# Block 2: the value projection in halves of 512 columns, from two pairs of weight tiles each

## The chip, the cores and the metric

One core of a Trainium2 chip runs the whole program. The metric is the device time of one execution, in microseconds; the time shown is the median of three runs. A TensorE matmul is written PE here, its weight load PEld, VectorE is DVE, ScalarE is ACT, GpSimd is POOL, and SP issues the DMAs.

## The reference, cut to what matters

The program computes two blocks, one behind the other, on x of 512 tokens and 1024 features, all in fp32. The first block is a mixer of softmax attention and a gated delta rule with a gated projection behind it. The second block has two layers:

```python
for i in range(2):
    h = rms_norm_2(x, attn_norm[i])
    if i % 2 == 0: mix = stick_breaking_mixer(h, w_in[i], w_out[i])     # 16 heads of 64
    else:          mix = diff_mixer(h, positions, w_in[i], w_out[i], ...) # 8 heads of 2*64, partial rope
    x = x + mix
    x = x + swiglu_ffn(rms_norm_2(x, ffn_norm[i]), w_gate[i], w_up[i], w_down[i])
```

In either layer w_in has 3072 columns: q, k and v of 1024 columns each. Attention is causal: stick-breaking weights in layer 0, the difference of two softmaxes in layer 1. The change concerns v = h @ w_in[:, 2048:3072] of both layers.

## The kernel before, in words

**Precision and the weights.** A product of fp32 matrices is made of three matmuls in the type fp32r: high part by high part, high by low, and low by high. The weights come in 149 tiles ("pairs") of 128 partitions by 2048 columns, each a DMA of 1 MB into `raw`, in two buffers. Each is split in four pieces of 512 columns: ACT writes the high part (`w_hi`), DVE the low part (`w_lo`), both into `spl`, also in two buffers. A pair can be split only when the matmuls of the pair before the last are done, since they read the same half of `spl`.

**Main matmuls.** Activations stand with features on the partitions (`hh` and `hl`, high and low, 8 tiles of 128x512). A block of a pair is a 128x128 piece of weights; `mul` steps hold it in the array and move 512 tokens past it. 8 blocks of 3 matmuls make one output tile of 128 features, and a pair has 16 blocks, so 48 matmuls. The value projection (`gemm_tok`, steps `tok`) is the other way about, because v is needed with tokens on the partitions: a 128x128 piece of `hh` or `hl` is held in the array and the weights move past it. Before, one pair holds 256 columns of v for all 8 contraction tiles; for each of four blocks of 128 tokens (`tb`) 24 matmuls of 256 columns fill half a PSUM bank, and `v_out` scales it into `v8`. Four such pairs make v of a layer. `V_BEHIND` tells behind which tiles m of q and k they stand: 0, 2, 4, 6 in layer 0 and 1, 3, 5, 7 in layer 1. The pair behind is split at the second block of tokens (`tb == 1`).

**The order.** `arrange` writes out one list of steps, and each engine issues its own steps in the order of that list. Main matmuls run through; lanes (one generator for each kind of side work, named in `LANES`) put steps between them when the clock that the planner keeps of each engine lets them in. The numbers in `LANES` (rank, slack, lag, tie) and the costs above (`CHANGE`: what a change between fp32r and fp32 matmuls is thought to cost) decide this. Where a main step needs an operand that no lane has made yet, `until` forces lanes on, so that all steps up to that operand stand in the list before the next main matmul.

**Attention of layer 0.** For each tile m (two heads): `st_q`, `st_k` take q and k out of PSUM, `st_z` ... `st_l` (front lane) and `st_w`, `st_t`, `st_x`, `st_f`, `st_o`, `st_a` (back lane) run over four key blocks. `st_o` multiplies with v and waits for `v_out` of that head's columns. `os_hi` (ACT) and `os_lo` (DVE, line 2627) split the result for the output projection.

**Attention of layer 1.** For each m: `br_in` (DVE line 2823), a DMA that turns rows (`br_dma`), `br_ss` (PE), `br_rot` (2834), `br_out` (2839, 2844); then for four query blocks `df_s` (PE, and a maximum on DVE, 2848), `df_p` (2855, 2859, 2861, 2863), `df_t` (transposes on PE, copied by DVE 2871 or ACT), then `df_o` (PE, with v), `df_n` (PE) and `df_out` (2877). Again `os_hi` and `os_lo`.

**Output projection.** `out_proj` makes the 8 output tiles in two halves: first contraction tiles 0 to 3 for all 8 outputs (96 matmuls), then 4 to 7; for outputs 0 and 1 the tile k = 7 comes last, behind 18 matmuls. In layer 1 the operand tile 3 lies in a buffer that the rope lane uses, so `split_lane` lets `os_hi`/`os_lo` of tile 3 and up run only behind `br_out` of k of tile 7.

## Time and profile before

| | us |
|---|---|
| median of 3 runs | 2134.86 |
| lowest, highest | 2133.43, 2135.09 |
| the profiled execution | 2137.93 |
| its span | 2136.1 |
| PE busy | 2099.5 (98%) |
| DVE busy | 1256.4 (59%) |
| ACT busy | 1066.0 (50%) |
| POOL busy | 228.8 (11%) |
| DMA, all queues | 87 GB/s mean, 186.89 MB |

The span runs from the first to the last instruction of one profiled execution. PE busy counts a matmul from its recorded start to its end, and matmuls overlap in the array: the pace of a stream is read from start to start, not from the length of one. The granted TensorE clock was 0.998 of full speed on average, that is the level of 2.4 GHz nearly throughout.

### The profile page before, as it was taken

Reading aid. Unit: us, or ns where it says so; the run is one execution under the profiler, and the core shown is the slowest. Engines: PE = TensorE matmul, PEld = TensorE weight load, DVE = VectorE, ACT = ScalarE, POOL = GpSimd, SP = SyncE. Lnnn points to the kernel's source line nnn. Section 1 sums busy time; section 2 is a strip of 40 time slices with the busy share of each in tenths; the row PEclk is TensorE's granted clock in tenths of the full one; section 3 lists DMA queues with packets and bytes.
Section 4 is the critical chain, followed back from the end, with each engine's and each line's share of the span. In section 5 each row is a group of like instructions: output and inputs, shape, how many; then the busy total and the mean of one; then the engine's idle time right before and its main releaser. Section 6 shows DMA issues by size and latency. Waiting matters only on the chain.

```text
span 2136.1 us, 36010 instructions
## 1 busy us (share of the span) xinstructions
PE 2099.5 (98%) x15046; PEld 1678.5 (79%) x15046; DVE 1256.4 (59%) x2218; ACT 1066.0 (50%) x2094; POOL 228.8 (11%) x240
## 2 busy tenths in 40 slices
PE   7999999999999999999999999999999999999999
PEld 6777877877778887877777888888777778888887
DVE  6776767766755555655567443444677775443442
ACT  6766756766755236656664332333455554322331
POOL 1213221322120010100011000000111101000000
PEclk9999999999999999999999999999999999999999
DMA  4322222121224332111112222222212112232222
GB/s 182 109 66 81 71 74 81 66 89 52 71 75 157 120 138 98 60 60 60 60 60 80 100 102 85 93 99 99 84 64 65 65 66 94 98 112 85 99 103 76
DMA packets 36227, 186.89 MB, mean 87 GB/s; under 512 B 4560, under 2 KB 4944, under 8 KB 16992
## 3 DMA queue, kind: packets, MB, share of 16 engines
q1 hardware_dynamic: 36064, 184.58, 25.2%
q8 instruction: 119, 1.95, 0.4%
q14 instruction: 44, 0.36, 0.1%
HBM read 173.00 MB, written 7.90 MB: 85 GB/s over the span
## 4 chain that ended last, share of the span: by engine, by line
PE 90%; DVE 5%; ACT 3%; issue 1%; DMA 0%; SPq 0%; POOL 0%; DVEq 0%; ACTq 0%
PE ps L1930 89%; PE ps L1933 1%; ACT arena L2882 1%; DVE spl L2388 1%; ACT spl L2885 1%; ACT hh L2882 0%; DVE x L2748 0%; DMA raw<-wstream 0%; DVE hl L2699 0%; DVE arena L2407 0%; DVE arena L2691 0%; DVE x L2677 0%; DVE arena L2673 0%; ACT arena_r L2882 0%; ACT pad L2882 0%
## 5 line engine op out<-in xcount | busy, mean ns | idle before, releaser
L1930 PE MATMUL ps<-hh,spl 128*128 128x512 f32 (+1 forms) x3152 | 1014.4, 395 | 7.1 <-DVE hl L2699 1.6
L1930 PEld LDWEIGHTS ps<-hh,spl 128*128 128x128 f32 x3152 | 585.9, 188 | 138.1 <-issue 14.8
L1930 PE MATMUL ps<-hl,spl 128*128 128x512 f32 (+1 forms) x1568 | 617.1, 394 | 0.0
L2388 DVE TENSOR_TENSOR spl<-raw,spl 128x512 fp32r<-128x512 f32 x596 | 422.1, 733 | 137.3 <-ACT spl L2885 136.0
L1930 PE MATMUL ps<-arena_r,spl 128*128 128x512 f32 x1968 | 466.8, 391 | 8.9 <-DVE arena_r L2400 8.4
L1930 PEld LDWEIGHTS ps<-arena_r,spl 128*128 128x128 f32 x1968 | 370.2, 188 | 89.9 <-issue 11.6
L2885 ACT ACTIVATE spl<-raw 128x512 fp32r<-128x512 f32 x596 | 344.6, 618 | 144.4 <-PE ps L1930 139.0
L1930 PEld LDWEIGHTS ps<-hl,spl 128*128 128x128 f32 x1568 | 295.2, 188 | 61.6 <-issue 6.4
L2882 ACT ACTIVATE arena<-arena 128x512 f32<-128x512 f32 (+3 forms) x204 | 132.1, 649 | 180.3 <-DVE arena L2753 139.4
L1930 PE MATMUL ps<-arena 32*32 32x32 f32 (+7 forms) x5664 | 216.4, 224 | 5.3 <-issue 5.1
L1930 PEld LDWEIGHTS ps<-arena 32*32 32x32 f32 (+4 forms) x5664 | 127.1, 115 | 80.1 <-issue 71.4
L2885 ACT ACTIVATE arena_r<-arena 128x512 fp32r<-128x512 f32 x64 | 40.4, 631 | 203.0 <-DVE arena L2760 193.6
L2748 DVE TENSOR_TENSOR x<-x,ps 128x512 f32<-128x512 f32 x64 | 43.8, 685 | 134.8 <-PE ps L1930 134.7
L2882 ACT ACTIVATE arena<-ps,small 128x512 f32<-128x512 f32 (+3 forms) x126 | 71.0, 566 | 87.9 <-DVE small L2848 45.7
L3369 POOL TENSOR_TENSOR arena<-arena 128x512 f32<-128x512 f32 x29 | 38.6, 1331 | 615.8 <-ACT arena L2882 615.8
L2882 ACT ACTIVATE arena<-ps 128x512 f32<-128x512 f32 (+5 forms) x116 | 68.2, 600 | 71.0 <-PE ps L1930 68.7
L1930 PE MATMUL ps<-spl,hh 128*128 128x256 f32 x512 | 97.1, 290 | 0.0
L2757 DVE TENSOR_TENSOR arena<-ps,arena 128x512 f32<-128x512 f32 x44 | 30.4, 691 | 104.4 <-PE ps L1930 104.4
L1930 PEld LDWEIGHTS ps<-spl,hh 128*128 128x128 f32 x512 | 80.2, 191 | 7.2 <-issue 6.3
L2753 DVE TENSOR_TENSOR arena<-ps,arena 128x512 f32<-128x512 f32 x44 | 30.4, 691 | 77.1 <-PE ps L1930 74.7
L1930 PE MATMUL ps<-spl,hl 128*128 128x256 f32 x256 | 72.3, 282 | 0.0
L3358 POOL TENSOR_SCALAR kdt<-arena,small 128x128 f32<-128x128 f32 x48 | 38.4, 811 | 280.7 <-PE ps L1930 280.7
(272 smaller groups left out, 2138.3 us busy)
## 6 DMA issues: line engine op xcount, KB each, us to landing
raw<-wstream SPq DMA_DIRECT2D x148, 1024.0 KB, 4.9
arena<-spill SPq DMA_DIRECT2D x17, 256.0 KB, 5.5
GS<-g_rows SPq DMA_DIRECT2D x16, 256.0 KB, 3.8
spill<-x SPq DMA_DIRECT2D x14, 256.0 KB, 2.0
arena<-arena SPq DMA_DIRECT2D x18, 128.0 KB, 2.1
x<-xT SPq DMA_DIRECT2D x4, 512.0 KB, 6.2
spill<-arena SPq DMA_DIRECT2D x8, 256.0 KB, 2.0
x<-xT SPq DMA_DIRECT2D x1, 2048.0 KB, 7.6
```

Source lines behind the costliest of these rows:

```text
L1930: return pe.matmul(out, lhsT, rhs, start=start, stop=stop, skip_group_check=True)
L1933: return pe.transpose(out, in_, C["ident"])
L2388: tt(spl[:, p % 2, 1, c], raw[:, p % 2, c], spl[:, p % 2, 0, c].bitcast(F32), ALU.subtract) \
L2748: tt(X[q.m], X[q.m], psum[q.u.b][:, :], ALU.add).then_inc(drained[q.u.b], 1)
L2753: tt(f_sl[q.i], psum[q.u.b][:, :], SQ[q.name][2], ALU.mult).then_inc(drained[q.u.b], 1)
L2757: tt(p, psum[q.u.b][:, :], SQ[q.g.name][2], ALU.mult).then_inc(drained[q.u.b], 1)
L2882: return act.activation(out, in_, func, **kw)
L2885: return act.activation(out, in_, ACT.Copy)
L3358: i = po.tensor_scalar(kdt[:, d, :], g4(keep_of[q.keep]["kt"])[:, c, :], g3(edec)[:, c, col:col + 1], None, ALU.mult)
L3369: tt(acc, acc, tmp[q.i], ALU.add).then_inc(sem("sq_pool"), 1)
```

## The change

The value projection of either layer is made in two halves of 512 columns instead of four parts of 256. A half has 512 columns for 8 contraction tiles, which is two pairs of weights: pair p holds contraction tiles 0 to 3, pair p + 1 tiles 4 to 7. Two blocks of tokens go together: both through pair p (12 matmuls each, of 512 columns), then both through pair p + 1, and then the other two blocks of tokens the same way. A semaphore `pairs` tells that pair p is done, so that pair p + 2 can be split over it. Pair p + 1 is split at the first four steps, pair p + 2 at the last pass but one. The halves stand behind tiles 1 and 4 of q and k, in both layers. `v_out` takes 512 columns at once, 16 in all instead of 32. `st_o` and `df_o` of tiles 0 to 3 use the first half of v and those of tiles 4 to 7 the second.

`CHANGE` goes from 0.088 to 0.02, `vmm` joins the kinds that are counted as fp32r, and all 28 rows of `LANES` are new, so the order of the side work is another one in the whole program, block 1 included.

```diff
-V_BEHIND = ((0, 2, 4, 6), (1, 3, 5, 7))
+V_BEHIND = ((1, 4), (1, 4))
-CHANGE = 0.088
-ONE_PASS = ("mul", "tok", "ar_ss", "cv_r", "on_b", "st_w", "st_t")
+CHANGE = 0.02
+ONE_PASS = ("mul", "tok", "vmm", "ar_ss", "cv_r", "on_b", "st_w", "st_t")
-    'att': (5, 3, 0.3, 0),
+    'att': (5, 1, 1, 0.5),
...
     def gemm_tok(op, done):
         o.flush()
         p, b = divmod(o.block, 16)
-        assert b == 0
-        for tb in range(4):
-            if tb == 1:
-                split(p + 1)
-            o.until(main.ready)
-            u = main.take()
-            o.clock["PE"] = max(o.clock["PE"], u.t, o.pair_t[p])
-            for q in range(4):
-                st = o.main("tok", p, tb, q, cost=[("PE", 0.72)])
...
+        for tbs in ((0, 1), (2, 3)):
+            us = {}
+            for half in range(2):
+                for tb in tbs:
+                    if half == 0:
+                        o.until(main.ready)
+                        us[tb] = main.take()
+                    u = us[tb]
+                    o.clock["PE"] = max(o.clock["PE"], u.t, o.pair_t[p + half])
+                    for k in range(4):
+                        if (tb, half) == (0, 0):
+                            split(p + 1, [k])
+                        if (tb, half) == (2, 1):
+                            split(p + 2, [k])
+                        st = o.main("vmm", p + half, tb, k, cost=[("PE", 3 * MUL)])
+                        st.pair_mark = (half, tb, k) == (0, 3, 3)
...
+                elif kind == "vmm":
+                    u, j, c = q.u, q.p % 2, slice(q.tb * 128, q.tb * 128 + 128)
+                    w.wait_ge(sem("w_lo"), 4 * q.p + q.k + 1)
+                    n = slice(512 * q.k, 512 * q.k + 512)
+                    mm(o, hi[:, c], spl[:, j, 0, n], q.half == 0 and q.k == 0, False)
+                    mm(o, hi[:, c], spl[:, j, 1, n], False, False)
+                    i = mm(o, lo[:, c], spl[:, j, 0, n], False, q.half == 1 and q.k == 3)
...
-            while ("v_out", 0, kb, m // 2) not in o.at or not obs.ready():
+            while ("v_out", 0, kb, m // 4) not in o.at or not obs.ready():
-        while ("v_out", 1, 3, m // 2) not in o.at or not obk.ready() or not on_slot.ready():
+        while ("v_out", 1, 3, m // 4) not in o.at or not obk.ready() or not on_slot.ready():
```

**Place 1, PE, the first value projection of layer 0.** `hh,spl` and `hl,spl` are main matmuls of q and k, `cst,arena 128x1` is `rs_col`, `spl,hh` and `spl,hl` are the value projection, `arena 128x...` with `mask_b` a score of the stick-breaking attention. Before:

```order
L1930 MATMUL ps<-hl,spl 128x256
L1930 MATMUL ps<-hh,spl 128x256
L1930 MATMUL ps<-cst,arena 128x1 x4
L1930 MATMUL ps<-spl,hh 128x256 x2
L1930 MATMUL ps<-spl,hl 128x256
```

And changed:

```order
L1940 MATMUL ps<-hl,spl 128x512
L1940 MATMUL ps<-hh,spl 128x512 x2
L1940 MATMUL ps<-hl,spl 128x512
L1940 MATMUL ps<-hh,spl 128x512
L1940 MATMUL ps<-cst,arena 128x1 x4
L1940 MATMUL ps<-spl,hh 128x512 x2
L1940 MATMUL ps<-spl,hl 128x512
```

The projection now stands behind the 512-column matmuls of tile 1, not behind tile 0, which is made in halves of 256 tokens; its own matmuls have 512 columns.

**Place 2, PE, the start of the output projection of layer 1.** The operands `GS_r`, `rv_r` belong to contraction tiles 0 to 2 of the attention's output, `arena_r` to the low parts and to tile 3. `cst,arena 128x128` are transposes (`df_t`), `arena,cst`, `pad,cst` and `on_t,cst` the sums of `br_ss` and `df_n`, `arena 128x...` x2 with `mask_b` the scores `df_s`. Before, the last of the value projection and the first of the output projection:

```order
L1930 MATMUL ps<-spl,hh 128x256 x2
L1930 MATMUL ps<-spl,hl 128x256
L1930 MATMUL ps<-GS_r,spl 128x512
L1930 MATMUL ps<-arena_r,spl 128x512
L1930 MATMUL ps<-GS_r,spl 128x512
L1933 MATMUL ps<-cst,arena 128x128 x4
L1930 MATMUL ps<-GS_r,spl 128x512
L1930 MATMUL ps<-arena_r,spl 128x512
L1930 MATMUL ps<-GS_r,spl 128x512
L1930 MATMUL ps<-rv_r,spl 128x512
```

Changed, from the last matmul with tile 2 to the first with tile 3 (27 rows lie between the last `hh,spl` of k of tile 7 and that one, of which these are the last):

```order
L1940 MATMUL ps<-rv_r,spl 128x512
L1943 MATMUL ps<-cst,arena 128x128
L1940 MATMUL ps<-arena 128x256 x2
L1940 MATMUL ps<-mask_b 128x64 x2
L1940 MATMUL ps<-pad,cst 128x512
L1940 MATMUL ps<-arena 128x384 x2
L1940 MATMUL ps<-mask_b 128x64 x2
L1943 MATMUL ps<-cst,arena 128x128 x2
L1940 MATMUL ps<-arena 128x512 x2
L1940 MATMUL ps<-mask_b 128x64 x2
L1943 MATMUL ps<-cst,arena 128x128 x3
L1940 MATMUL ps<-on_t,cst 128x512
```

Before, the last 96 matmuls of the value projection lie between k of tile 7 and the output projection. Now the output projection starts right behind k of tile 7, and eleven rows of side work without a main matmul among them stand ahead of its tile 3.

On DVE, the end of what stands there from `br_in` of k of tile 7 to the `os_lo` of tile 3 that the same matmul needs: 29 instructions before, 25 changed. Before:

```order
L2848 TENSOR_REDUCE small<-ps 128x2
L2871 COPY arena<-ps 128x3x128
L2705 TENSOR_SCALAR arena<-ps,small 128x256
L2834 TENSOR_TENSOR on_t<-on_t,arena 128x512
L2855 RECIPROCAL small<-small 128x2
L2859 TENSOR_TENSOR small<-small 128x2
L2861 TENSOR_SCALAR arena<-arena,small 128x512
L2863 SCALAR_TENSOR_TENSOR arena<-arena,small 128x512
L2839 TENSOR_TENSOR pad<-pad,on_t 128x512
L2844 TENSOR_TENSOR arena<-pad 128x512
L2848 TENSOR_REDUCE small<-ps 128x2
L2627 TENSOR_TENSOR arena_r<-arena,arena_r 128x512
```

And changed:

```order
L2873 TENSOR_REDUCE small<-ps 128x2
L2859 TENSOR_TENSOR on_t<-on_t,arena 128x512
L2864 TENSOR_TENSOR pad<-pad,on_t 128x512
L2869 TENSOR_TENSOR arena<-pad 128x512
L2873 TENSOR_REDUCE small<-ps 128x2
L2880 RECIPROCAL small<-small 128x2
L2884 TENSOR_TENSOR small<-small 128x2
L2886 TENSOR_SCALAR arena<-arena,small 128x384
L2888 SCALAR_TENSOR_TENSOR arena<-arena,small 128x384
L2896 COPY arena<-ps 128x3x128
L2652 TENSOR_TENSOR arena_r<-arena,arena_r 128x512
```

The chain on DVE is of the same kinds and about as long; the weight splits and the `v_out` that stood in it are gone, and what PE has to do beside it is less.

**Place 3, PE, the last attention tile of layer 0 in the output projection.** `rv_r,const_r`, `st_r,const_r` and `arena_r,const_r 128x128` are `st_w` and `st_t` of tile 7, last key block; `arena 64x128 x2` is its `st_o`. `arena_r,spl` are the matmuls of the output projection. Before:

```order
L1930 MATMUL ps<-rv_r,const_r 128x128
L1930 MATMUL ps<-st_r,const_r 128x128
L1930 MATMUL ps<-arena_r,const_r 128x128 x2
L1930 MATMUL ps<-arena_r,spl 128x512 x5
L1930 MATMUL ps<-arena 64x128 x2
L1930 MATMUL ps<-arena_r,spl 128x512 x88
L1930 MATMUL ps<-hh,spl 128x512
```

And changed:

```order
L1940 MATMUL ps<-rv_r,const_r 128x128
L1940 MATMUL ps<-st_r,const_r 128x128
L1940 MATMUL ps<-arena_r,const_r 128x128 x2
L1940 MATMUL ps<-arena 64x128 x2
L1940 MATMUL ps<-arena_r,spl 128x512 x78
L1940 MATMUL ps<-hh,spl 128x512
```

The last 78 matmuls begin with k = 7 of outputs 0 and 1. Before, five matmuls stood ahead of `st_o` and ten between it and k = 7; now none stands at either place.

## Rows read from the trace of the kernel before

**Rows 1.** The page: busy time, share and instructions of PE; the chain by engine.

```profile
PE 2099.5 (98%) x15046; PEld 1678.5 (79%) x15046; DVE 1256.4 (59%) x2218; ACT 1066.0 (50%) x2094; POOL 228.8 (11%) x240
...
PE 90%; DVE 5%; ACT 3%; issue 1%; DMA 0%; SPq 0%; POOL 0%; DVEq 0%; ACTq 0%
```

**Rows 2.** Timeline of PE in a value projection: start, us, instruction.

```profile
1714.06 0.40 PE L1930 MATMUL ps<-spl,hh 128*128 128x256 f32 x2
...
1715.86 0.40 PE L1930 MATMUL ps<-spl,hh 128*128 128x256 f32 x2
```

**Rows 3.** Timeline of PE in the FFN, 512 columns, nothing between.

```profile
1805.27 0.39 PE L1930 MATMUL ps<-hl,spl 128*128 128x512 f32 x1
...
1808.67 0.39 PE L1930 MATMUL ps<-hl,spl 128*128 128x512 f32 x1
```

**Rows 4.** Timeline of PE ahead of the first value projection.

```profile
891.23 1.02 PE L1930 MATMUL ps<-cst,arena 128*128 128x1 f32 x8 [0.82 <-ACT arena L2882]
```

**Rows 5.** Windows: us, PE, PEld, DVE, ACT, POOL busy, clock, DMA share, GB/s.

```profile
1701.28:1719.97 18.69, 18.69 (x135) 15.48 (x134) 15.83 (x29) 9.77 (x25) 1.77 (x1) 1.00 0.19 60
```

**Rows 6.** Timeline of DVE in that stretch and just behind it.

```profile
1705.78 0.48 DVE L2705 TENSOR_SCALAR arena<-ps,small 128x256 f32<-128x256 f32 x1
1706.63 3.60 DVE L2388 TENSOR_TENSOR spl<-raw,spl 128x512 fp32r<-128x512 f32 x4 [0.37 <-ACT spl L2885]
...
1714.35 0.68 DVE L2834 TENSOR_TENSOR on_t<-on_t,arena 128x512 f32<-128x512 f32 x1
...
1716.01 0.75 DVE L2863 SCALAR_TENSOR_TENSOR arena<-arena,small 128x512 f32<-128x512 f32 x1
...
1718.95 0.42 DVE L2848 TENSOR_REDUCE small<-ps 128x2 f32<-128x256 f32 x1 [0.86 <-PE ps L1930]
1719.29 0.68 DVE L2627 TENSOR_TENSOR arena_r<-arena,arena_r 128x512 fp32r<-128x512 f32 x1
...
1720.97 0.35 DVE L2863 SCALAR_TENSOR_TENSOR arena<-arena,small 128x128 f32<-128x128 f32 x1
1721.89 0.29 DVE L2871 COPY arena<-ps 128x128 f32<-128x128 f32 x1 [0.57 <-PE ps L1933]
1722.79 0.69 DVE L2848 TENSOR_REDUCE small<-ps 128x2 f32<-128x512 f32 x1 [0.60 <-PE ps L1930]
```

**Rows 7.** Timeline of PE, layer 1: side work of each kind.

```profile
1702.60 0.92 PE L1930 MATMUL ps<-arena 64*128 64x384 f32 x4
...
1708.78 1.02 PE L1930 MATMUL ps<-pad,cst 128*128 128x512 f32 x2
1709.24 0.80 PE L1930 MATMUL ps<-spl,hh 128*128 128x256 f32 x2
...
1716.92 0.61 PE L1933 MATMUL ps<-cst,arena 128*128 128x128 f32 x4
1717.29 0.47 PE L1930 MATMUL ps<-GS_r,spl 128*128 128x512 f32 x1
...
1719.18 2.32 PE L1930 MATMUL ps<-arena 128*128 128x512 f32 x8
1721.26 0.49 PE L1930 MATMUL ps<-rv_r,spl 128*128 128x512 f32 x1
```

**Rows 8.** Timeline of PE and DVE, end of the attention of layer 0.

```profile
1126.70 1.71 PE L1930 MATMUL ps<-arena_r,spl 128*128 128x512 f32 x5
1126.80 0.53 ACT L2882 ACTIVATE arena<-ps 128x256 f32<-128x256 f32 x2
...
1128.34 0.44 PE L1930 MATMUL ps<-arena 128*64 128x128 f32 x4
1128.70 3.93 PE L1930 MATMUL ps<-arena_r,spl 128*128 128x512 f32 x16
...
1129.88 0.69 DVE L2627 TENSOR_TENSOR arena_r<-arena,arena_r 128x512 fp32r<-128x512 f32 x1
```

**Rows 9.** Windows: most of block 1.

```profile
50.00:600.00 550.00, 538.36 (x6831) 427.27 (x6831) 386.26 (x750) 375.58 (x783) 126.78 (x131) 0.99 0.23 77
```

More of the change, by code:

```diff
@@ L384, in gemm_tok @@
         p, b = divmod(o.block, 16)
-        assert b == 0
-        for tb in range(4):
-            if tb == 1:
-                split(p + 1)
-            o.until(main.ready)
-            u = main.take()
-            o.clock["PE"] = max(o.clock["PE"], u.t, o.pair_t[p])
-            for q in range(4):
-                st = o.main("tok", p, tb, q, cost=[("PE", 0.72)])
-                st.u, st.op, st.p, st.tb, st.q = u, op, p, tb, q
-                st.need = None if tb else [op.ready[k] for k in (2 * q, 2 * q + 1) if k not in op.seen]
-                op.seen |= {2 * q, 2 * q + 1}
-                if q < 3:
+        assert b == 0 and all(k in op.seen for k in range(KT))
+        for tbs in ((0, 1), (2, 3)):
[13 more added lines that the diff above has]
+                        st = o.main("vmm", p + half, tb, k, cost=[("PE", 3 * MUL)])
+                        st.u, st.op, st.p, st.tb, st.half, st.k = u, op, p + half, tb, half, k
+                        st.pair_mark = (half, tb, k) == (0, 3, 3)
+                        if k < 3:
+                            o.step()
+                    if half == 1:
+                        done(tb, u)
+                    elif tb == 3:
+                        o.n_pair_marks += 1
+                        o.pair_done[p] = ("pairs", o.n_pair_marks)
                     o.step()
-            done(tb, u)
-            o.step()
-        o.pair_done[p] = ("bank", u)
-        o.block += 16
+        o.pair_done[p + 1] = ("bank", u)
+        o.block += 32
     def low(op, k, kind, *key, then=None):
@@ L1226, in done @@
         def done(tb, u):
-            st = o.main("v_out", layer, tb, j, cost=[("AC" if tb % 2 else "DV", 0.4)])
+            st = o.main("v_out", layer, tb, j, cost=[("AC", AC_B) if tb % 2 else ("DV", DV_B)])
             st.u, st.tb, st.j, st.layer = u, tb, j, layer
@@ L1574, in arrange @@
         o.spawn("score", score_lane(m))
-        behind = [("df_out", m)] + [("br_out", "k", 7)] * (m > 2) + [("v_out", 1, 3, 3)] * (m == 7)
+        behind = [("df_out", m)] + [("br_out", "k", 7)] * (m > 2) + [("v_out", 1, 3, 1)] * (m == 7)
         o.spawn("split", split_lane("ob", ob, m, behind))
@@ L1979, in tensor @@
                         i.then_inc(filled[u.b], 1)
+                elif kind == "vmm":
+                    u, j, c = q.u, q.p % 2, slice(q.tb * 128, q.tb * 128 + 128)
+                    if q.k == 0 and q.half == 0 and u.n > 1:
+                        w.wait_ge(drained[u.b], u.n - 1)
+                    w.wait_ge(sem("w_lo"), 4 * q.p + q.k + 1)
+                    n = slice(512 * q.k, 512 * q.k + 512)
+                    hi, lo = HI[q.op.hi][4 * q.half + q.k], HI[q.op.lo][4 * q.half + q.k]
+                    o = psum[u.b][:, :]
+                    mm(o, hi[:, c], spl[:, j, 0, n], q.half == 0 and q.k == 0, False)
+                    mm(o, hi[:, c], spl[:, j, 1, n], False, False)
+                    i = mm(o, lo[:, c], spl[:, j, 0, n], False, q.half == 1 and q.k == 3)
+                    if q.pair_mark:
+                        i.then_inc(sem("pairs"), 1)
+                    elif q.half == 1 and q.k == 3:
+                        i.then_inc(filled[u.b], 1)
                 elif kind == "norm":
@@ L3133, in scalar @@
                         if k == 7:
-                            full(at["v_out", 1, 3, 3].u)
+                            full(at["v_out", 1, 3, 1].u)
                     copy(HI[name + "_h"][k], o8[k]).then_inc(sem("os_hi"), 1)
@@ L3474, in lay_out @@
             if m in V_BEHIND[i]:
-                tm(w, 2048 + 256 * V_BEHIND[i].index(m), 1)
+                c = 2048 + 512 * V_BEHIND[i].index(m)
+                for k in range(0, 8, 4):
+                    out.append(w[128 * k:128 * k + 512, c:c + 512].reshape(4, 128, 512).transpose(1, 0, 2).reshape(128, 2048))
         fm(a["w_out_2"][i], 0, 8, 0, OUT_FIRST)
```

68 lines of the change are left out of this document (34 added, 34 removed).

## The prediction

> **What bounds the kernel now.** I read the page first: PE is busy for 98% of the span, the next engine (DVE) for 59%, and the chain that ended last lies on PE for 90% [rows 1]. The reader is to see there that only two things change the time: the pace of PE's own stream, and the 36.6 us (2136.1 less 2099.5) in which PE stands still, so a microsecond saved on DVE or ACT counts only where PE waits for it. The timeline gives the pace of the two kinds of matmul that the change exchanges. Then I looked where PE waits now and where it would wait: at the first value projection, where attention ends in either layer, and in block 1. The order of the instructions tells what stands where; all durations are from the trace.
>
> **The value projection's own matmuls.** In a stream of 256 columns a matmul starts every 0.120 us: 15 of them between 1714.06 and 1715.86 [rows 2]. With 512 columns it is 0.227: 15 between 1805.27 and 1808.67 [rows 3], at full clock. Before there are 2 layers x 4 pairs x 96 = 768 matmuls of 256 columns, 768 x 0.120 = 92.2 us. Now there are 2 x 2 halves x 96 = 384 of 512, 384 x 0.227 = 87.2 us. All of it is on PE, so it counts in full: minus 5.0. The trace has no 512-column matmul with weights as the moving operand. The bounds are the rows' 0.227 and twice 0.120: a gain between 5.0 and 0. I take 5.0, because 256 columns cost the same 0.12 in either role in the rows I saw.
> For this exchange the Trainium skill (TensorE: Matmul & The Clock Gate, section Back-to-back issue gap) gives a spacing of N / 2.4 + 2.5 ns, so that only 2.5 ns per matmul is fixed. By it the gain would be 384 x 2.5 ns = 1.0 us; the rows have 120 and 227, so twice 120 less 227 is 13 ns, and the measurement decides.
>
> **The first projection no longer waits.** `rs_col` of layer 0 stands idle for 0.82 us for an ACT result of the norm [rows 4], since it follows tile 0 at once. Behind tile 1, 10.9 us (48 x 0.227) later, that result is old. Minus 0.8. `v_out` has half as many instructions, off the path: nothing.
>
> **Splits inside the projection.** Pair p + 1 must be split during the first 24 matmuls, 5.4 us, where before there was the whole of tb 1 to 3 (72 x 0.12 = 8.6 us). Four splits in a row took 3.60 us on DVE [rows 6], so 1.8 us is left for what stands between them on DVE and ACT. The wait is finer now (one piece of 512 columns at a time), which covers most. Eight such places (two per half): between 0 and 1 us each; I take 0.3 in all, with 8 as the bad end.
>
> **The start of the output projection in layer 1.** This is where I see a new wait. Before, the fourth value projection (96 x 0.12 = 11.5 us of PE) stands between k of tile 7 and the output projection. Now nothing does, and after nine main matmuls PE comes to contraction tile 3, whose `os_lo` is behind `br_out` of k of tile 7. It is the only place in block 2 where the order puts more than a dozen steps of DVE and ACT between two main matmuls.
> The chain on DVE: from `br_in` to that `os_lo` before took 18.69 us, 15.83 of them busy (85%), with PE never idle [rows 5]. Out of the 15.83 go the four weight splits (3.60) and two `v_out` (0.48 each), which leaves 11.3 [rows 6]. The softmax step there is of 128 instead of 512 columns (0.35 for 0.75, and I estimate 0.2 on the instruction ahead of it), and added are one `br_rot` (0.68), one copy (0.29) and a maximum of 512 for one of 256 columns (0.69 for 0.42): 11.3 - 0.6 + 1.24 = 11.9 us. It starts where the maximum of the first score of tile 6 is done. Ahead of that PE has five main matmuls (1.14), a sum (0.86), four transposes (0.45) and a score (0.6), 3.1 us, and the maximum takes 0.42: 3.5 us behind k of tile 7. So `os_lo` ends at 3.5 + 11.9 = 15.4 us if DVE never waits, and at 3.5 + 11.9 / 0.85 = 17.5 us if it waits as often as before.
> PE's work until then [rows 7]: nine main matmuls 2.0; three sums, each 0.86 (0.46 to the next start, whose record is 0.40 longer than usual), 2.6; ten transposes at 0.11 (four: 0.37 to the next start and 0.08 on its record), 1.1; `df_o` 2.08 and 0.09, 2.2; four scores, 384 columns at 0.92 and, by steps of 0.2 about it, 3.4. Together 11.3 us. PE waits 15.4 - 11.3 = 4.1 to 17.5 - 11.3 = 6.2 us. I take 5.2. Behind the waiting matmul stands the whole output projection, so nothing hides it; lanes that got ahead meanwhile save nothing later, since PE did not wait there before.
>
> **The end of attention in layer 0.** Before, five main matmuls stand ahead of the last `st_o` and ten behind it, ahead of k = 7. Now none does. Before: `st_w`/`st_t` end about 1126.9, `st_x`/`st_f` on ACT at 1127.33, `st_o` starts 1128.34 behind the five matmuls and is done by 1128.8, and `os_lo` ends at 1130.57 [rows 8]. Without them PE waits 0.5 us for ACT and then from the end of `st_o` to that of `os_lo`, 1130.57 - 1128.78 = 1.8. Together 2.3. The ends: 1.5, if `os_hi` and `os_lo` come without the 0.6 us split that stood ahead, and 3.5, if the scores are late as well.
>
> **The rest of the order.** The new lanes move all side work. The matmuls of block 1 are the same, and PE's idle time there is what can change: 550 - 538.36 = 11.6 us in the stretch from 50 to 600 us [rows 9]. I counted in the two lists of steps the places in block 1 where PE's side work stands behind a step of another engine with no main matmul between: 104 before, 86 now. In proportion 11.6 x 18 / 104 = 2.0 us less. The ends: 7 less (0.6 of it gone), 5 more, since such a list can just as well lose. PE changes between fp32r and fp32 work 375 times instead of 350. The 0.08 us that a main matmul behind transposes is longer on record [rows 7] is mostly theirs; I estimate 0.02 for a change: plus 0.4.
>
> **The sum.** -5.0 - 0.8 + 0.3 + 5.2 + 2.3 - 2.0 + 0.4 = +0.4 us. The profiled execution had 2137.93 us, its span 2136.1; the sum on it is 2138.3. The median of the runs is 3.1 us lower, so the forecast is 2134.86 + 0.4 = 2135.3 us.
>
> **Rivals.**
> *Block 1 gains more* (faster). The costs of the planner and the new lanes fit the chip better, and 7 of the 11.6 idle us go. For it: the 104 places that became 86, and that PE's idle time is spread over many short waits. Against it: the same lane numbers must serve both blocks, and the list of block 2 got a wait worse than any before. With the wait in layer 1 at its lower end (4.1): 2135.3 - 5.0 - 1.1 = 2129.2 us.
> *The chain in layer 1 takes what it took before* (slower). Its 25 instructions alternate with ACT, so taking the weight splits out of DVE need not shorten it: they filled gaps. If it takes 18.7 us again, PE waits 3.5 + 18.7 - 11.3 = 10.9 us instead of 5.2: 2141.0. It is slower than a measurement can miss as soon as the chain takes more than 17 us (wait 9.2). For it: 85% busy was with splits in the gaps. Against it: PE work between (scores, sums) came late before because main matmuls stood ahead of it, and now comes at once.
> *The splits are late* (slower). If each of the eight places costs 1 us, because maxima and softmax steps stand between them, 2135.3 + 7.7 = 2143.0. For it: DVE is 75 to 85% busy in layer 1. Against it: raw weights are long there, and each piece is waited for alone.
> *The 512-column form gains nothing*: weights as the moving operand at 0.24 each. Then 2140.3. Little speaks for it.
>
> **How the numbers follow.** A measurement of this kernel can tell 0.2%, 4.3 us, so "faster" is under 2130.6 and "slower" over 2139.1. Forecast as it stands, with its parts inside their bounds: 0.45. Block 1 gains more: 0.27. Chain as long as before: 0.15. Late splits: 0.09. No gain by 512 columns: 0.04. That gives 0.27 faster, 0.45 same, 0.28 slower. The likeliest case alone has a range of 2131 to 2139. For 8 in 10, I go down to the first rival's side, 2128, and up past the second rival to 2142.
>
> **What would show it.** The value projections have 384 matmuls of 512 columns, 0.227 apart: any other pace fails the first step. PE should show no wait for ACT ahead of `rs_col` of layer 0. PE should be idle for 4 to 6 us in short waits in the 18 us behind k of tile 7 of layer 1, the last of them ended by `os_lo` on DVE; if PE is busy there throughout, the main loss is wrong and the kernel is faster by 5 us. PE should be idle for 2.3 us at the end of the attention of layer 0. Idle time between 50 and 600 us should be near 9.6 us; far from it, the term that I know least has decided.

## The result, and the profile after

| | before | changed |
|---|---|---|
| median of 3 runs, us | 2134.86 | 2149.25 |
| lowest, highest | 2133.43, 2135.09 | 2146.03, 2149.97 |
| profiled execution, its span | 2137.93, 2136.1 | 2149.25, 2147.5 |
| PE busy | 2099.5 | 2097.7 |
| attention of layer 0 | 242.2 | 250.0 |
| attention of layer 1 | 239.7 | 248.4 |
| PE idle in layer 0's attention | 1.4 | 5.2 |
| PE idle in layer 1's attention | 2.5 | 11.2 |

The changed kernel is slower: the ratio of the medians is 1.0065, with an interval of 1.0051 to 1.0079. The forecast was 2135.3 with a range up to 2142.

The page of the changed kernel, the two rows that answer to [rows 1]:

```profile
PE 2097.7 (98%) x14662; PEld 1657.7 (77%) x14662; DVE 1262.6 (59%) x2210; ACT 1062.1 (49%) x2086; POOL 231.5 (11%) x240
...
PE 86%; DVE 7%; ACT 4%; issue 1%; DMA 1%; SPq 0%; POOL 0%; DVEq 0%; ACTq 0%
```

PE is busy 1.8 us less, but it stands still for 49.8 us (2147.5 - 2097.7) instead of 36.6, and of the 4% of the chain that PE lost, 3% went to DVE and ACT and 1% to DMA.

To find where, I took the start of the same main matmul in both traces, stage by stage. Block 1 takes 4.9 us less, the norm behind it 0.3 less, the attention of layer 0 (from the norm to the first output of contraction tiles 4 to 7) 7.8 more, the feed-forward network of layer 0 0.1 less, the attention of layer 1 8.8 more, and the rest the same: +11.3 on the profiled executions, whose times differ by 11.32. All of the loss is in the two attention stages.

**v.** The timeline of PE in the first projection (start, us, instruction), for [rows 2, 3], and the group of `rs_col`, for [rows 4]:

```profile
898.01 0.95 PE L1940 MATMUL ps<-cst,arena 128*128 128x1 f32 x8
...
900.45 0.62 PE L1940 MATMUL ps<-spl,hh 128*128 128x512 f32 x2
900.90 0.39 PE L1940 MATMUL ps<-spl,hl 128*128 128x512 f32 x1
...
902.26 0.39 PE L1940 MATMUL ps<-spl,hl 128*128 128x512 f32 x1
```

From 900.45 to 902.26 there are eight steps from start to start, 0.226 us each, and `rs_col` has no idle time ahead of it. Both steps came as forecast. The brackets below hold idle time only, from the recorded end of one matmul to the start of the next. A record is 0.16 us longer than the pace and the first matmul behind a wait takes about 0.1 more, so a wait costs 0.2 to 0.3 us beside its idle time.

**Layer 0.** The timeline of PE and DVE at the two places in the projections where PE waited; in brackets idle time and its releaser:

```profile
910.82 0.75 DVE L2730 TENSOR_SCALAR arena<-ps,small 128x512 f32<-128x512 f32 x1 [2.06 <-PE ps L1940]
...
911.72 1.08 PE L1940 MATMUL ps<-arena 128*64 128x512 f32 x4 [0.94 <-DVE arena L2730]
...
932.87 0.75 DVE L2730 TENSOR_SCALAR arena<-ps,small 128x512 f32<-128x512 f32 x1
...
933.76 0.65 PE L1940 MATMUL ps<-arena 128*64 128x256 f32 x4 [1.70 <-DVE arena L2730]
```

L2730 is `v_out`. The new order has a `st_o` as the very next PE instruction behind the last matmul of a block of v, so PE waits for DVE to take that block out of PSUM. In the second case DVE was also at weight splits and came to `v_out` 0.8 us after the block was done. At the end of the stage, for [rows 8]:

```profile
1130.09 0.44 PE L1940 MATMUL ps<-arena 128*64 128x128 f32 x4
...
1130.97 0.63 ACT L2910 ACTIVATE arena_r<-arena 128x512 fp32r<-128x512 f32 x1 [0.68 <-DVE arena L2768]
...
1131.63 0.69 DVE L2652 TENSOR_TENSOR arena_r<-arena,arena_r 128x512 fp32r<-128x512 f32 x1 [0.70 <-ACT arena_r L2910]
1132.37 3.91 PE L1940 MATMUL ps<-arena_r,spl 128*128 128x512 f32 x9 [1.84 <-DVE arena_r L2652]
```

This is the forecast wait: 2.0 us idle (0.12 and 1.84), where the forecast had 2.3. The kernel before had a wait of 0.5 us in this part, at 1125.8, so the term is 1.5 us net. Windows over it and over the wait at 933 (last columns: granted clock, DMA share, GB/s):

```profile
930.00:940.00 10.00, 8.30 (x34) 6.41 (x35) 5.71 (x13) 3.58 (x8) 0.42 (x1) 0.83 0.29 105
...
1131.00:1136.00 5.00, 3.63 (x9) 2.77 (x10) 2.03 (x4) 2.32 (x4) 0.00 (x0) 0.66 0.00 0
```

The granted clock is under 1: 0.83 over 10 us and 0.66 over 5 us are each 3.4 us at the lower level of 1.2 GHz, right behind a wait of 1.7 and of 1.8 us. In [rows 8] there was no wait. I had not thought of the clock at all.

Idle time in this stage is 5.2 us instead of 1.4, and 6.2 us at half clock lie inside it, worth 3.1 us at most. With v 2.5 us quicker, that makes 4.4 of the 7.8 us. The other 3.4 are in the stream itself. PE goes from main matmuls to those of `st_z` or `st_o` and back 55 times instead of 42. These use half of the array (`64*128` or `128*64` in the rows); e9 below has the price of such a visit. No edit in layer 0 shows that the 3.4 us are these 13 visits.

**Layer 1.** The timeline of PE from k of tile 7 (its last matmul starts 0.23 us ahead of the first row, which is the first matmul of the output projection) to contraction tile 3, for [rows 5, 7]:

```profile
1708.50 0.43 PE L1940 MATMUL ps<-GS_r,spl 128*128 128x512 f32 x1
1709.18 1.10 PE L1940 MATMUL ps<-arena,cst 128*128 128x512 f32 x2 [0.25 <-ACT arena L2907]
...
1714.90 0.48 PE L1940 MATMUL ps<-rv_r,spl 128*128 128x512 f32 x1
...
1716.08 1.13 PE L1940 MATMUL ps<-pad,cst 128*128 128x512 f32 x2
1717.99 0.92 PE L1940 MATMUL ps<-arena 64*128 64x384 f32 x4 [0.78 <-ACT arena L2907]
...
1720.39 0.44 PE L1943 MATMUL ps<-cst,arena 128*128 128x128 f32 x2 [1.46 <-DVE arena L2888]
1722.53 1.68 PE L1940 MATMUL ps<-arena 64*128 64x512 f32 x4 [1.69 <-ACT arena L2907]
...
1727.04 0.87 PE L1943 MATMUL ps<-cst,arena 128*128 128x128 f32 x3 [2.78 <-DVE arena L2888]
...
1729.16 0.83 PE L1940 MATMUL ps<-arena_r,spl 128*128 128x512 f32 x1
```

Four waits, 6.7 us, and 0.25 us at 1709, none of them for `os_lo` itself: PE's own side work (score, transposes, score, transposes) is part of the chain and is late each time, for an exponential on ACT or the end of a softmax on DVE. The two score matmuls on `64x512` took 1.68 us at half clock. DVE between, for [rows 6]:

```profile
1712.47 0.68 DVE L2848 TENSOR_TENSOR pad<-ps,arena 128x512 f32<-128x512 f32 x1
...
1717.21 1.40 POOL L3408 TENSOR_TENSOR pad<-pad,st 128x512 f32<-128x512 f32 x1 [3.49 <-DMA on_t<-pad]
1717.52 1.65 DVE L2869 TENSOR_TENSOR arena<-arena 128x512 f32<-128x512 f32 x1
...
1724.30 1.22 DVE L2873 TENSOR_REDUCE small<-ps 128x2 f32<-128x1024 f32 x1 [0.97 <-PE ps L1940]
...
1728.43 0.68 DVE L2652 TENSOR_TENSOR arena_r<-arena,arena_r 128x512 fp32r<-128x512 f32 x1
```

And the window from that `br_in` to that `os_lo`:

```profile
1712.47:1729.11 16.64, 9.92 (x40) 4.59 (x38) 13.05 (x27) 8.72 (x24) 2.65 (x2) 0.82 0.02 4
```

The chain took 16.6 us; it was 18.69 before [rows 5], but hidden. DVE was busy for 13.05 of it (78%), where the forecast had 11.9 and 85% at worst. 1.0 of the 1.1 us too much is one `br_out` (L2869): 1.65 us while POOL worked, 0.69 elsewhere. PE ran at half clock from 1723.0 to 1729.8, 6.8 us. From k of tile 7 to tile 3 it is 20.7 us (1729.16 less 1708.50). With the 11.3 us that the forecast gave to PE's own work, 9.4 us are lost, where it had 5.2: 7.0 us of idle time, and the rest clock, restarts and what 11.3 was short. Earlier in the stage three more waits of 0.95, 0.78 and 0.78 us stand at 1543, 1572 and 1656, which before did not have; the first is ahead of the first matmul of v, for a `br_in`.

**Block 1.** The window that answers to [rows 9]:

```profile
50.00:600.00 550.00, 537.88 (x6857) 429.37 (x6856) 397.66 (x755) 373.26 (x784) 129.64 (x133) 1.00 0.23 77
```

PE idles for 12.1 us, not for 9.6 as forecast and 11.6 before. What changed is the clock, 1.00 for 0.99: the execution profiled before had two pieces of 3.4 us at half clock (at 49.6 and 107.6 us), this one none. Two later executions of the same block 1 instructions without any, e8 and e11 below, were 4.0 and 2.9 us quicker in it than that profile. So 3 to 4 of the 4.9 us come and go between executions, and the order brought 1 to 2. That is also why the medians differ by 14.4 us and the profiles by 11.3.

### The profile page after: what moved, and what is told of

It is laid out like the page before. It is cut to its first block, busy times and chain, and to the rows that moved or that the text cites. A ratio compares the mean times of both kernels' runs of the same rounds, so it can differ in the third digit from the quotient of the medians.

```text
span 2147.5 us, 35252 instructions
## 1 busy us (share of the span) xinstructions
PE 2097.7 (98%) x14662; PEld 1657.7 (77%) x14662; DVE 1262.6 (59%) x2210; ACT 1062.1 (49%) x2086; POOL 231.5 (11%) x240
## 4 chain that ended last, share of the span: by engine, by line
PE 86%; DVE 7%; ACT 4%; issue 1%; DMA 1%; SPq 0%; POOL 0%; DVEq 0%; ACTq 0%
PE ps L1940 85%; ACT arena L2907 2%; PE ps L1943 1%; DVE spl L2413 1%; ACT spl L2910 1%; DMA arena<-spill 1%; DVE x L2773 0%; ACT hh L2907 0%; DMA raw<-wstream 0%; DVE hl L2724 0%; DVE arena L2432 0%; DVE arena L2716 0%; DVE x L2702 0%; DVE arena L2698 0%; ACT on_t L2907 0%
## 5 line engine op out<-in xcount | busy, mean ns | idle before, releaser
L1940 PEld LDWEIGHTS ps<-hh,spl 128*128 128x128 f32 x3152 | 584.3, 188 | 142.2 <-issue 14.4
L1940 PE MATMUL ps<-arena_r,spl 128*128 128x512 f32 x1968 | 471.6, 393 | 10.6 <-DVE arena_r L2425 8.4
L1940 PEld LDWEIGHTS ps<-arena_r,spl 128*128 128x128 f32 x1968 | 371.2, 189 | 95.3 <-issue 14.4
L1940 PE MATMUL ps<-spl,hh 128*128 128x512 f32 x256 | 84.0, 409 | 1.0 <-DVE pad L2848 1.0
L2910 ACT ACTIVATE arena<-ps 128x256 f32<-128x256 f32 (+2 forms) x88 | 39.3, 448 | 52.5 <-PE ps L1940 41.0
L1940 PEld LDWEIGHTS ps<-spl,hh 128*128 128x128 f32 x256 | 46.2, 189 | 17.5 <-issue 6.9
```

Of the source, the lines that this page charges most:

```text
L1940: return pe.matmul(out, lhsT, rhs, start=start, stop=stop, skip_group_check=True)
L2910: return act.activation(out, in_, ACT.Copy)
```

## The experiments

Two theories stood at the start. A: v's last block between k of tile 7 and the output projection was cover for the attention of tiles 5 to 7, and taking it away is the loss. B: the new lanes, made with a charge of 0.02 for a change of type, are the loss. The stage times below are those of one profile each, and waits are idle time as in the brackets.

### Width alone, and order alone (e1, e2)

e1 is the changed kernel with the old charge and lanes, e2 the kernel before with the new ones.

```diff
 e1, against the changed kernel
-CHANGE = 0.02
+CHANGE = 0.088
-    'att': (5, 1, 1, 0.5),
+    'att': (5, 3, 0.3, 0),
...
 e2, against the kernel before
-CHANGE = 0.088
+CHANGE = 0.02
-    'att': (5, 3, 0.3, 0),
+    'att': (5, 1, 1, 0.5),
...
```

> The changed kernel with the old LANES and the old CHANGE (0.088): the new value projection alone. The order again puts 22 steps of side work between two main matmuls in front of contraction tile 3 of the output projection of layer 1. Theory A (the place of v makes the wait there, and a wait that long halves TensorE's clock for a while): a wait of 7 to 11 us there, with a granted clock of 0.5 in it, and +3 to +9 us against before. Theory B (the new lane numbers are the fault): no slower than before, by the projection's gain 2130 us.

> The kernel before with the new LANES and CHANGE 0.02, and v as it was. Theory A: no wait in layer 1; block 1 is 4.9 us shorter as in the changed kernel; in all 2128 to 2134 us, unless the end of the attention of layer 0 (20 steps in one place in this order) costs 4 us and a dip of the clock. Theory B: +8 us or more against before.

e1: 2156.12 us, ratio 1.0099 (1.0084 to 1.0114). Layer 0 +4.7 us with 56 groups on half the array, layer 1 +16, with 11.0 us idle between 1716 and tile 3 at 1734.8 and 13.7 us at half clock from 1727.5 on. e2: 2154.72 us, 1.0090 (1.0075 to 1.0105): layer 0 +7.5 with 54 groups, layer 1 +12.5 with waits of 4.0 us at 1731 to 1733 and 2.1 at 1773. Each half of the change alone costs 19 to 20 us, both together 14. They don't add; the new lanes suit the new v better than the old lanes do, and neither is good. Neither theory stands alone. In e1 the wait of A came, in a total far above A's 3 to 9 us, and B fell. In e2 it is the other way: A had 2128 to 2134 us and B 8 us or more, and B came. There the last quarter of v still stands behind tile 7 and layer 1 is 12.5 us longer all the same, so the new lanes can lose as much in it with the cover in place.

### v's second half back behind tile 7 (e3)

```diff
-V_BEHIND = ((1, 4), (1, 4))
+V_BEHIND = ((1, 4), (1, 7))
```

> The changed kernel with the second half of v of layer 1 behind tile 7 of q and k instead of tile 4, so that 21.8 us of matmuls stand again between k of tile 7 and the output projection. Theory A: the wait of 8.8 us and the 6.8 us at half clock in front of contraction tile 3 go, 8 to 10 us faster than the changed kernel, about 2139 to 2141. Theory B (the wait only moves to where df_o of tiles 4 to 7 needs v): 3 us faster at most.

2168.31 us, 1.0155 (1.0140 to 1.0170), the slowest of all: layer 1 +27. The cover is there, but half a v is the columns of four tiles. `df_o` of tiles 4 to 7 now waits for it. PE waits 1.9, 3.5, 2.8 and 4.5 us at 1625 to 1699, as I read it because q and k find no free slot, and 8.2 us in four waits at 1771 to 1781. My expectation was wrong; the test changed more than the cover, and decides nothing on A.

### Spare matmuls in the waits (e4)

Matmuls of 320 columns whose results are overwritten, 10 and 19 of them, ahead of two of the transposes that waited.

```diff
+                    if m == 6 and qb in (1, 2):
+                        for _ in range(10 if qb == 1 else 19):
+                            mm(psum[u.b][:, 0:320], ones_r[:, :], const_r[:, :], True, True)
```

> The changed kernel with 29 spare matmuls of 320 columns (constants, into the bank that the transposes then overwrite) put in front of two transposes of tile 6 of layer 1, where PE waited 1.46 and 2.78 us: about 0.146 us each, so 1.5 and 2.8 us of work in place of idle time. If the half clock follows from PE being idle, the 6.8 us at 0.5 there shorten or go, and 1 to 3.4 us are won; if the loss is the chain on DVE alone, the time stays or grows by up to 1 us.

2146.93 us, 1.0051 (1.0034 to 1.0068), for 2149.25. The window of the stretch in e4:

```profile
1710.00:1731.00 21.00, 18.13 (x100) 12.20 (x99) 17.27 (x35) 12.94 (x34) 2.68 (x2) 1.00 0.03 6
```

The clock is 1.00 there, for 0.82, and the stage takes 1.3 us less (247.1). So the clock was worth about 1.3 us of the 9.4. The waits for the chain on DVE and ACT remain: tile 3 still comes 19.8 us behind k of tile 7.

### Buffers of their own for tiles 3 to 5 (e5, e7)

Theory C: it is only the dependence of `os_hi`/`os_lo` of tile 3 on `br_out` of k of tile 7, through a shared buffer.

```diff
-        behind = [("df_out", m)] + [("br_out", "k", 7)] * (m > 2) + [("v_out", 1, 3, 1)] * (m == 7)
+        behind = [("df_out", m)] + [("br_out", "k", 7)] * (m > 5) + [("v_out", 1, 3, 1)] * (m == 7)
-        HI["ob_h"] = [...] + [R(i) for i in (20, 21, 22)] + [...]
+        HI["ob_h"] = [...] + [R(i) for i in (41, 42, 43)] + [...]
...
-                        if k > 2:
+                        if k > 5:
                             w.wait_ge(sem("br_out"), 16)
```

> The changed kernel with contraction tiles 3, 4 and 5 of the output projection's operand of layer 1 in buffers of their own, so that their os_hi and os_lo wait only for their own df_out and not for br_out of k of tile 7. Theory A (the 8.8 us ahead of tile 3 are a false dependence through that buffer, made late by the place of v): they go, and of the 11.3 us that the output projection of layer 1 ends late at least 6 do; about 2141 to 2143 us, with some 2 us of a new wait at k = 7. Theory C (the attention of tiles 6 and 7 itself is late, whichever buffer it has): the wait moves to k = 7 with its full size and the time stays within 2 us of the changed kernel's.

2155.33 us, 1.0090 (1.0073 to 1.0107), 6 us slower than the changed kernel. PE passes tile 3 without a wait, and then waits for tiles 6 and 7, 9.2 us in six waits from 1748 to 1771 with 12.8 us at half clock. Two of them:

```profile
1751.48 0.44 PE L1943 MATMUL ps<-cst,arena 128*128 128x128 f32 x2 [1.10 <-DVE arena L2888]
...
1754.93 0.79 PE L1940 MATMUL ps<-pad_r,spl 128*128 128x512 f32 x1 [1.92 <-DVE arena_r L2652]
...
1766.30 1.13 PE L1940 MATMUL ps<-on_t,cst 128*128 128x512 f32 x2 [1.26 <-ACT arena L2907]
...
1770.98 0.79 PE L1940 MATMUL ps<-hh,spl 128*128 128x512 f32 x1 [3.55 <-DVE arena_r L2652]
```

The buffer is not the cause, since the loss does not go with it. Theory C had the time within 2 us of the changed kernel's; it came 6 us above. My reading, which no edit tests: what is late is the attention of the last tiles, and without the early stop the projection uses up the main matmuls under which it would have run. e7 is the same with the charge of 0.088:

> Both: tiles 3 to 5 in buffers of their own, and CHANGE 0.088. Theory A: neither the wait ahead of tile 3 nor that at the end of layer 0; 5 to 9 us faster than the changed kernel, 2140 to 2144 us, with about 2.5 us left at k = 7. If it comes under 2135 the value projection's 5 us reach the total.

2167.35 us, 1.0149 (1.0134 to 1.0164), layer 1 at 256.9 us, with 9.6 us of waits at 1760 to 1780 for the same tiles and 12.8 us at half clock. The forecast of 2140 to 2144 was far off.

### The charge alone (e6)

```diff
-CHANGE = 0.02
+CHANGE = 0.088
```

> The changed kernel with CHANGE back at 0.088. The order has 11 steps of side work in one place ahead of tile 3 (17 in the changed one) and none at the end of layer 0, and 58 groups of narrow matmuls (st_z, st_o) among the main ones of layer 0 instead of 55. If waits decide: 2 to 4 us gone at the end of layer 0 and 2 to 4 in layer 1, about 2142 us. If the number of groups decides, at 0.2 us each: +0.6 us in layer 0 beside that. If the order of block 1 decides: block 1 ends more than 3 us later or earlier.

2164.33 us, 1.0131 (1.0116 to 1.0146). Block 1 +11.1 us, layer 0 +3.6 (0.5 us of wait at its end), layer 1 +11.0. Of the three forecasts the one on block 1 came: the lanes were made for the charge of 0.02, and with another they give a poor order there.

### What a wait does to the clock (e8)

The kernel before, with 9 to 18 spare products on DVE ahead of five of the `f_g` of the dense feed-forward network of layer 1.

```diff
+                    for _ in range({(0, 2): 9, (0, 5): 11, (0, 8): 13, (1, 2): 18, (1, 6): 10}.get(q.key[1:], 0) if q.key[0] else 0):
...
+                        tt(A(41), A(42), A(42), ALU.mult).then_inc(pad_ops.sem, pad_ops.up())
```

> The kernel before with 9, 11, 13, 18 and 10 spare products of 512 columns on DVE ahead of five f_g of the FFN of layer 1, so that PE, otherwise dense there, stands still about 1, 2.5, 3.5, 6.5 and 2 us at five places. If idle time of PE alone brings the half clock, each gap over 2.5 us is followed by at least 3.4 us at 0.5, and the kernel is longer by the gaps and 1.7 us more for each 3.4 us at 0.5; the shorter gaps show where it begins. If only long mixed stretches bring it, the granted clock stays at 1.0 and the kernel is longer by the gaps alone, about 15 us.

One run, 2158.99 us. Two of the four waits in the timeline of PE in e8, and windows of 10 us behind them:

```profile
1804.36 0.47 PE L1930 MATMUL ps<-hh,spl 128*128 128x512 f32 x1 [2.24 <-DVE spl L2388]
...
1840.94 0.77 PE L1930 MATMUL ps<-hh,spl 128*128 128x512 f32 x1 [3.69 <-DVE spl L2388]
```

```profile
1836.00:1846.00 10.00, 6.31 (x21) 4.82 (x20) 7.27 (x12) 3.34 (x6) 0.00 (x0) 0.83 0.31 105
1802.00:1812.00 10.00, 7.76 (x35) 6.37 (x35) 6.08 (x10) 4.49 (x8) 0.00 (x0) 1.00 0.32 107
```

Behind 2.2 us of idle time the clock stayed, behind 3.7 us it was halved for 3.4 us, and with 5.1 and 6.2 us for 6.8 each, of which the first 2.1 us fell into the wait itself. The network took 25.5 us more, 17.8 of it idle. The other 7.7 go with 12.8 us in which PE worked at half clock: halving is 6.4 of them, and restarts behind four waits about 1. In the attention stages the clock fell after less: behind the wait of 1.7 us at 933 in three executions that share that stretch (the changed kernel, e4, e10), and not in two others (e3, e5), whose layer 0 was about 1.5 us quicker.

### What a group on half the array costs (e9)

The kernel before with spare fp32 matmuls of 128 columns ahead of 100 output tiles of the network, 1, 2 or 4 at a time.

```diff
+                        for _ in range(times):
+                            if form == 0:
+                                mm(o[:, 0:128], C["ident"][0:64, :], C["ones"][0:64, :], True, True)
+                            elif form == 1:
+                                mm(o[0:64, 0:128], C["ident"][:, 0:64], C["ones"], True, True)
+                            elif form == 2:
+                                mm(o[:, 0:128], C["ident"], C["ones"], True, True)
```

> The kernel before, with spare fp32 matmuls of 128 columns ahead of the first matmul of 100 output tiles of the feed-forward network (50 in each layer), in groups of 1, 2 or 4: on 64 rows of the array (as st_z), on 64 columns of it (as st_o), or on all of it. Theory (each return from a half array to the whole one costs about 0.2 us, whatever the size of the group): the time added at a start, set against the group's size, has an intercept of about 0.2 us for the two half forms and below 0.05 us for the whole one. Rival (it is the spare matmuls themselves, or the change of type, that cost): the intercept is the same for all three forms.

The timeline of PE in e9 round a pair of each form (an fp32 matmul has two records):

```profile
1158.78 0.39 PE L1930 MATMUL ps<-hh,spl 128*128 128x512 f32 x1
1159.10 0.71 PE L1930 MATMUL ps<-cst 64*128 64x128 f32 x4
1159.74 0.50 PE L1930 MATMUL ps<-hh,spl 128*128 128x512 f32 x1
...
1177.88 0.39 PE L1930 MATMUL ps<-hh,spl 128*128 128x512 f32 x1
1178.19 0.65 PE L1930 MATMUL ps<-cst 128*64 128x128 f32 x4
1178.78 0.50 PE L1930 MATMUL ps<-hh,spl 128*128 128x512 f32 x1
...
1196.56 0.39 PE L1930 MATMUL ps<-hh,spl 128*128 128x512 f32 x1
1196.78 0.60 PE L1930 MATMUL ps<-cst 128*128 128x128 f32 x4
1197.14 0.48 PE L1930 MATMUL ps<-hh,spl 128*128 128x512 f32 x1
```

From main matmul to main matmul it is 0.96, 0.90 and 0.58 us. Over all starts, the time added by 1, 2 and 4 spares (median of 8 to 10 each, over four main matmuls of 0.227 around them) is 0.63, 0.85, 1.30 us on 64 rows; 0.57, 0.81, 1.23 on 64 columns; 0.24, 0.46, 0.91 on the whole array. Every spare costs 0.22 in each form; what remains for the group is 0.40, 0.35 and 0.02. The form of the theory holds, its size does not: I had 0.2 us for a visit to half the array, and it is 0.35 to 0.40. A change of type costs 0.02 us, as I had it. The Trainium skill (TensorEngine Tiling (Array Packing), Key Properties) says that a change of the tiling mode drains the engine, and gives no price. By these, the 13 groups more in layer 0 would be 4.6 to 5.2 us; 3.4 are left for them there.

### A short softmax (e10, e11)

In both kernels the softmax of tiles 5, 6 and 7 of layer 1 works on a quarter of its columns (the rest is left out), in the same order.

```diff
-                    n, i = 128 * q.key[1] + 128, 2 * ((q.n - 1) % 8)
+                    n, i = (128 * q.key[1] + 128) // (4 if q.key[0] > 4 else 1), 2 * ((q.n - 1) % 8)
```

> The changed kernel, with the softmax of tiles 5, 6 and 7 of layer 1 on a quarter of its columns (VectorE and ScalarE work on 32 to 128 columns for 128 to 512; the rest is left out, the order stays). Theory (these tiles' chain on VectorE and ScalarE is what TensorE waits for ahead of contraction tile 3, and the half clock follows from the wait): idle time of TensorE in attention layer 1 falls from 11.2 to under 4 us, no half clock there, the stage goes from 248.4 to 237 to 240 us, the time to 2138 to 2141. Rival (the order that TensorE itself was given costs it there): the stage stays above 244 us.

> The kernel before with the same cut. Theory: its stage of 239.7 us holds 4.1 us of waits, of which the cut takes 3 at most: 236.5 to 239 us, and the changed kernel with the cut is then 0 to 2 us quicker than it in this stage, which is what v alone brings there (2.0). Rival (the chain costs both kernels alike): it gains as much as the changed kernel does.

e10: 2145.51 us, 1.0051 (1.0034 to 1.0068); its layer 1 takes 245.3 us, over my bound of 244 for the rival, and PE is idle there for 8.0 us, not for under 4. e11: 2135.39 us, 1.0003 (0.9994 to 1.0013), layer 1 at 239.6: nothing gained. The waits of e10:

```profile
1717.78 0.92 PE L1940 MATMUL ps<-arena 64*128 64x384 f32 x4 [0.31 <-ACT arena L2907]
...
1720.01 0.44 PE L1943 MATMUL ps<-cst,arena 128*128 128x128 f32 x2 [1.28 <-DVE arena L2888]
...
1721.06 1.69 PE L1940 MATMUL ps<-arena 64*128 64x512 f32 x4 [0.62 <-ACT arena L2907]
...
1724.34 0.88 PE L1943 MATMUL ps<-cst,arena 128*128 128x128 f32 x3 [1.54 <-DVE arena L2888]
```

The same four waits, 3.8 us for 6.7, and again 6.8 us at half clock. Work on 32 columns instead of 128 still took 0.24 and 0.25 us for 0.29 and 0.35 on DVE, and the rope steps stay. So the length of the softmax carries under half of the wait, and the clock fell in either case. I put the rest down to the number of steps that take turns between engines; no run here changes that number alone.

### The lanes made anew at the old charge (e12)

The planner has a clock of its own. At a charge of 0.088 it had put e1 18 us and e6 32 us above the kernel before, and 20 and 28.5 were measured. So I had new lanes made at 0.088 for the new v, and the planner put the best 5 us above the kernel before.

```diff
-V_BEHIND = ((1, 4), (1, 4))
-CHANGE = 0.02
+V_BEHIND = ((1, 5), (2, 5))
+CHANGE = 0.088
+    (28 other rows of LANES)
```

> v in halves of 512 columns as in the changed kernel, with the planner's charge for a change of type back at 0.088 and its table of lanes made anew at that charge; v behind tiles 1 and 5 (layer 0) and 2 and 5 (layer 1). Theory (the new table was made at too low a charge, under which the planner could not see what its order costs): by the planner's own clock, which put v alone at 18 us and the charge alone at 32 us above the kernel before (20.3 and 28.5 measured), this order ends 5 us above it: 2138 to 2143 us, under the changed kernel and above the kernel before. Rival (v in halves of 512 columns does not suit this attention, however it is ordered): 2148 us or more. A version better than both would be under 2133 us.

2158.10 us, 1.0108 (1.0091 to 1.0125): +23, not +5. Block 1 +3.3, layer 0 +5.3 with 56 groups, layer 1 +9.7, with 4.1 us of waits at 1734 to 1744. The theory fell, and the time is in the rival's range; that no order suits the new v is not shown by one more. Its agreement on two kernels was no test of it: an order that is sought by a model finds the model's errors. Every order of the new v that ran with its full softmax has 247 us or more in layer 1.

### The last quarter alone (e13)

The kernel before, with v in quarters, and only the last quarter of layer 1 one tile earlier.

```diff
-V_BEHIND = ((0, 2, 4, 6), (1, 3, 5, 7))
+V_BEHIND = ((0, 2, 4, 6), (1, 3, 5, 6))
```

> The kernel before, v in its four quarters of 256 columns, only the last quarter of layer 1 moved from behind tile 7 of q and k to behind tile 6; nothing else (the width, the charge and the lanes stay). Layer 0 and block 1 have to stay as they were. Theory (what layer 1 lost is the 11.5 us of v between the last k and the output projection, under which the attention of tiles 5 to 7 ran): TensorE waits 5 to 10 us in the 20 us ahead of contraction tile 3, partly at half clock, and the stage of 239.7 us grows by 6 to 14 us. Rival (the last quarter covers nothing; the width of 512 or the new order is what costs there): it grows by under 3 us.

2146.01 us, 1.0054 (1.0038 to 1.0071). Layer 0 is unchanged (242.2 us) and layer 1 takes 249.3 for 239.7. The waits of PE in e13, and a window over them:

```profile
1718.44 2.42 PE L1930 MATMUL ps<-arena 128*128 128x512 f32 x8 [1.25 <-ACT arena L2885]
...
1722.04 0.49 PE L1930 MATMUL ps<-arena 64*128 64x128 f32 x4 [1.18 <-DVE arena L2844]
...
1726.68 0.92 PE L1930 MATMUL ps<-arena 64*128 64x384 f32 x4 [1.27 <-ACT arena L2882]
...
1730.45 0.69 PE L1933 MATMUL ps<-cst,arena 128*128 128x128 f32 x2 [2.83 <-DVE arena L2863]
```

```profile
1714.00:1734.00 20.00, 12.71 (x53) 6.30 (x51) 11.00 (x26) 9.90 (x25) 1.77 (x1) 0.85 0.08 26
```

Six waits with 7.3 us idle between 1718 and 1731 (four are shown) and 6.8 us at half clock, at the same place, with the old width, the old charge and the old lanes; the waits earlier in the stage are within 0.4 us those of the kernel before. That shows theory A's mechanism by one edit: 11.5 us of v at that place hid 9.6 us. It does not show that the changed kernel's loss in layer 1 is this alone, since e2 lost 12.5 us there by its lanes.

## Why the prediction was wrong

**v, -5.0.** Right in pace (0.226), which is 2.5 us in either layer. The spacing rule of the Trainium skill (TensorE: Matmul & The Clock Gate, Back-to-back issue gap) that the prediction sets beside it is given there for a matmul by itself; these streams have a weight load for each matmul, and the fixed part is 13 to 14 ns, not 2.5.

**The wait of `rs_col`, -0.8; the splits, +0.3.** The first is gone; no wait for a split shows in the projections of v.

**The start of the output projection in layer 1, +5.2 (4.1 to 6.2).** This step failed by its size. The mechanism was right, as e13 shows, but by the forecast's own subtraction 9.4 us were lost, not 5.2. The chain began 4.0 us behind k of tile 7 (1712.47 less 1708.50), where I had 3.5, and took 16.6 us, not "11.9 us" to 11.9 / 0.85 = 14.0. The 85% came from a stretch in which PE never waited and its side work was there in time [rows 5]; with PE, ACT and DVE taking turns it was 78%, a `br_out` beside POOL took 1.0 us longer, and PE's own part of the chain ran at half clock (1.3 us by e4). So `os_lo` ended 20.6 us behind k of tile 7, where I had 15.4 to 17.5. The rival with the chain at its old 18.7 us overstated the chain by 2.1 us and left out the clock; its 2141.0 is nearer than the forecast, and still has none of the losses of layer 0.

**The end of attention in layer 0, +2.3.** Nearly right (2.0 idle, 1.5 more than before), but without the 3.4 us at half clock behind it, up to 1.7 us.

**"I estimate 0.02 for a change: plus 0.4."** This step failed for layer 0. 0.02 is right for a change of type, as e9 has it (25 changes more make 0.5, not 0.4), but I counted 375 changes for 350 as one kind, and 13 visits more go to half the array at 0.35 to 0.40 each. What the stage leaves for them is 3.4 us.

**The rest of the order, -2.0 (-7 to +5).** I took it from block 1 alone. There the order brought 1 to 2 us, so the number came near, but by luck: it was to come from idle time, which did not fall. In layer 0 it put `st_o` right behind `v_out`, 2.6 us of waits and up to 1.7 of clock, which the order of the instructions shows and I did not price.

**The clock.** It stands in no term. It is at most 1.7 us at each of two places in layer 0 and about 1.3 in layer 1: up to 4.7 us.

By stage: layer 0 is 7.8 us longer (v -2.5, idle time +3.8, clock +3.1, and 3.4 left for the stream). Layer 1 is 8.8 longer (v -2.5, idle time +8.7, clock +1.3, and 1.3 left, at least in part what eight new waits cost beside their idle time). Block 1 and the norm are 5.2 shorter, the network of layer 0 is 0.1 shorter. That makes the 11.3 between the profiles.

## What to carry to other kernels

Before a block of matmuls is moved, ask what ran under it: its place may be worth more than its matmuls (here 9.6 us for a quarter of v whose new form saves 0.6). Where an uncovered chain takes turns between engines, do not price it by the busy share of a covered stretch (78% here for 85%); its number of turns is my guess for a better measure. Add the clock that its waits cost. Count separately the groups of matmuls that use half of the array: each costs 0.35 to 0.40 us beside its own work, where a change of type alone costs 0.02.
